# The order of rounding and shifting in the layer norms of a hybrid encoder trunk

## The reference

```python
def layer_norm(x, g, b):
    xf = x.astype(jnp.float32)
    mu = jnp.mean(xf, axis=-1, keepdims=True)
    var = jnp.mean(jnp.square(xf - mu), axis=-1, keepdims=True)
    return ((xf - mu) * lax.rsqrt(var + LN_EPS) * g + b).astype(x.dtype)

for l in range(DEPTH):                                      # DEPTH = 2, D_MODEL = 1024
    x = layer_norm(ALPHA * x + 0.5 * swiglu_ffn(x, ...), ln_g[l, 0], ln_b[l, 0])
    x = layer_norm(ALPHA * x + mix, ln_g[l, 1], ln_b[l, 1])  # mix of even_mixer or odd_mixer
    x = layer_norm(ALPHA * x + 0.5 * swiglu_ffn(x, ...), ln_g[l, 2], ln_b[l, 2])
```

## Time and profile before

| | |
|---|---|
| median of 3 runs | 2367.24 us (2366.89 to 2369.07) |
| the profiled execution | 2367.52 us |
| its span, first to last instruction | 2365.7 us |
| mean granted TensorE clock | 0.998 of full speed |
| TensorE busy | 2340.5 us, 99% |
| VectorE busy | 1701.5 us, 72% |
| ScalarE busy | 1157.2 us, 49% |
| GpSimd busy | 592.3 us, 25% |

### The profile page before, as it was taken

One profiled execution on the slowest core, in us unless ns is written; L12 is line 12 of the kernel. 1 busy time (PEld: TensorE's weight loads), 2 busy tenths in 40 slices (PEclk: granted clock), 3 DMA queues, 4 the chain that ended last, 5 costly groups with the idle time before them and its releaser, 6 DMA issues.

```text
span 2365.7 us, 40265 instructions
## 1 busy us (share of the span) xinstructions
PE 2340.5 (99%) x15948; PEld 2055.4 (87%) x15948; DVE 1701.5 (72%) x2228; ACT 1157.2 (49%) x1664; POOL 592.3 (25%) x310
## 2 busy tenths in 40 slices
PE   9999999999999999999999999999999999999998
PEld 8989987777788989989989988888888888998997
DVE  7818768998779728769728665798987547962857
ACT  5525537985446525536525534455554334552543
POOL 2040044001241030141030144333333334013013
PEclk9999999999999999999999999999999999999999
DMA  5333232232123333223333323222222222333332
GB/s 172 101 108 101 88 114 78 80 87 72 54 88 101 95 109 108 91 88 112 94 99 108 98 98 91 81 72 81 81 81 72 80 77 85 108 94 110 110 98 73
DMA packets 64720, 220.98 MB, mean 93 GB/s; under 512 B 11066, under 2 KB 15674, under 8 KB 64414
## 3 DMA queue, kind: packets, MB, share of 16 engines
q1 hardware_dynamic: 64542, 218.47, 29.8%
HBM read 216.35 MB, written 2.10 MB: 92 GB/s over the span
## 4 chain that ended last, share of the span: by engine, by line
PE 87%; DVE 9%; ACT 1%; issue 1%; POOL 1%; DMA 0%; SPq 0%; ACTq 0%; DVEq 0%
PE ps L735 13%; PE ps L737 13%; PE ps L736 13%; PE ps L920 11%; PE ps L921 11%; PE ps L919 11%; PE ps L717 2%; PE ps L723 2%; PE ps L718 2%; DVE sb_x L2433 1%; PE ps L1374 1%; DVE sb_wl L2567 1%; DVE sb_x L2425 1%; DVE sb_x L2437 1%; PE ps L1433 1%
## 5 line engine op out<-in xcount | busy, mean ns | idle before, releaser
L621 POOL TENSOR_TENSOR sb_low<-sb_src,sb_hi 128x1408 fp32r<-128x1408 f32 x60 | 194.9, 3249 | 1086.3 <-ACT sb_hi L1551 1086.2
L621 POOL TENSOR_TENSOR sb_wl<-sb_raw,sb_wh 128x1024 fp32r<-128x1024 f32 x114 | 284.9, 2499 | 518.6 <-ACT sb_wh L1551 494.8
L2242 DVE TENSOR_TENSOR sb_low<-sb_src,sb_hi 128x1024 fp32r<-128x1024 f32 (+1 forms) x304 | 329.5, 1091 | 71.7 <-ACT sb_hi L1615 60.8
L1615 ACT ACTIVATE sb_hi<-sb_src 128x1024 fp32r<-128x1024 f32 (+1 forms) x304 | 286.1, 947 | 186.0 <-PE ps L921 100.4
L919 PE MATMUL ps<-sb_tt,sb_hi 128*128 128x256 f32 x1216 | 344.1, 283 | 0.0
L920 PE MATMUL ps<-sb_tt,sb_low 128*128 128x256 f32 x1216 | 344.1, 283 | 0.0
L921 PE MATMUL ps<-sb_tt,sb_hi 128*128 128x256 f32 x1216 | 344.1, 283 | 0.0
L1551 ACT ACTIVATE sb_wh<-sb_raw 128x1024 fp32r<-128x1024 f32 x139 | 147.0, 1058 | 253.5 <-PE ps L737 222.2
L920 PE MATMUL ps<-sb_xh,sb_low 128*128 128x256 f32 x912 | 258.1, 283 | 0.0
L921 PE MATMUL ps<-sb_xl,sb_hi 128*128 128x256 f32 x912 | 258.1, 283 | 0.0
L919 PE MATMUL ps<-sb_xh,sb_hi 128*128 128x256 f32 x912 | 258.1, 283 | 0.0
(11 more groups left out here) (419 smaller groups left out, 5116.4 us busy)
## 6 DMA issues: line engine op xcount, KB each, us to landing
sb_src<-w_s SPq DMA_DIRECT2D x76, 768.0 KB, 4.3
sb_src<-w_out SPq DMA_DIRECT2D x64, 704.0 KB, 4.1
sb_raw<-w_od SPq DMA_DIRECT2D x80, 512.0 KB, 3.6
sb_raw<-w_ev SPq DMA_DIRECT2D x40, 512.0 KB, 3.7
sb_src<-w_s SPq DMA_DIRECT2D x76, 256.0 KB, 2.9
sb_src<-w_in SPq DMA_DIRECT2D x16, 512.0 KB, 3.6
sb_raw<-w_evo SPq DMA_DIRECT2D x8, 512.0 KB, 3.6
sb_raw<-w_odo SPq DMA_DIRECT2D x8, 512.0 KB, 3.7
```

The lines of the kernel that those rows point to most:

```text
L621: pool.tensor_tensor(sl.wl[:, 0:n], sl.raw[:, 0:n], sl.wh[:, 0:n].bitcast(F32), ALU.subtract).then_inc(lo_done, 1)
L1615: act.activation(hi[:, lo_:hi_at, :], groups(i)[g], ACT.Copy).then_inc(hi_s[g], 1)
L2242: dve.tensor_tensor(low[:, a_:b_, :], groups(i)[g], hi[:, a_:b_, :].bitcast(F32), ALU.subtract).then_inc(lo_s[g], 1)
```

## The change

Both engines' norms are reordered; the arithmetic of each value stays, except that the rounded part of an odd tile is now made from scaled tile plus bias on ScalarE, as it was for even tiles, and no more copied from the shifted tile. On ScalarE `tile` writes the rounded part of every tile, and a new `shift` adds the bias to `x` for even tiles, three tiles later in the first sequence (`SHIFT_BEHIND`) and one tile later in the second. On VectorE `tile` only scales, and a new `shift` adds the bias for odd tiles, three tiles later in the first sequence (tiles 5 and 7 after tile 7) and one tile later in the second; it waits for the rounded part to be there, since it writes over the tile that ScalarE reads. The low parts of odd tiles now wait for VectorE's shift as well. The last norm keeps its order.

```diff
--- before.py
+++ after.py
@@ -43,6 +43,7 @@
 CW = 32
 BY_ACT = (0, 2, 4, 6)
 BY_DVE = tuple(k for k in range(KD) if k not in BY_ACT)
+SHIFT_BEHIND = 3
 SUB_POOL = (4, 5, 6, 7)
 LOW_DVE = (4, 7)
 LOW_POOL = tuple(k for k in range(KD) if k not in LOW_DVE)
@@ -646,6 +647,8 @@
                     pool.wait_ge(xh_done, KD * g + k + 1)
                     if n and k in BY_ACT:
                         pool.wait_ge(x_act, len(BY_ACT) * (g - SEQS) + upto(BY_ACT, k))
+                    elif n:
+                        pool.wait_ge(x_dve, len(BY_DVE) * (g - SEQS) + upto(BY_DVE, k))
                     pool.tensor_tensor(xl[:, k, part(q)], x[:, k, part(q)], xh[:, k, part(q)].bitcast(F32),
                                        ALU.subtract).then_inc(xl_pool, 1)
 
@@ -1745,15 +1748,16 @@
                 def tile(q, k):
                     m = SEQS * ln + q
                     x_k, h_k, b = x[:, k, part(q)], xh[:, k, part(q)], vc("ln_b", ln * KD + k)
-                    if k in BY_ACT or not more:
-                        act.wait_ge(scaled, KD * m + k + 1)
-                        if more:
-                            act.activation(h_k, x_k, ACT.Identity, bias=b).then_inc(xh_done, 1)
-                            act.wait_ge(xh_done, KD * (m + SEQS) + k + 1)
+                    act.wait_ge(scaled, KD * m + k + 1)
+                    if more:
+                        act.activation(h_k, x_k, ACT.Identity, bias=b).then_inc(xh_done, 1)
+                    else:
                         act.activation(x_k, x_k, ACT.Identity, bias=b).then_inc(x_act, 1)
-                    elif more:
-                        act.wait_ge(x_dve, len(BY_DVE) * m + upto(BY_DVE, k))
-                        act.activation(h_k, x_k, ACT.Copy).then_inc(xh_done, 1)
+
+                def shift(q, k):
+                    m, x_k = SEQS * ln + q, x[:, k, part(q)]
+                    act.wait_ge(xh_done, KD * (m + SEQS) + k + 1)
+                    act.activation(x_k, x_k, ACT.Identity, bias=vc("ln_b", ln * KD + k)).then_inc(x_act, 1)
 
                 def mean(q):
                     act.wait_ge(mean_mm, 3 * ln + 2 + q)
@@ -1770,6 +1774,8 @@
                 rstd(0)
                 for k in range(KD):
                     tile(0, k)
+                    if more and k - SHIFT_BEHIND in BY_ACT:
+                        shift(0, k - SHIFT_BEHIND)
                     if k == 0:
                         last(1)
                     if k == 1:
@@ -1781,9 +1787,12 @@
                     if k == 7:
                         rstd(1)
                 if more:
+                    shift(0, BY_ACT[-1])
                     split(KD, next_slot(ln, 2), stages[ln + 1][1] + 2)
                 for k in range(KD):
                     tile(1, k)
+                    if more and k - 1 in BY_ACT:
+                        shift(1, k - 1)
 
             def head_rstd(c, r, ahead=None):
                 ln_and_exp()
@@ -2432,8 +2441,11 @@
                         dve.wait_ge(sub_done, (own_ + KD) * ln + own_ * q + k + 1)
                     dve.scalar_tensor_tensor(x_k, x_k, vc("ln_g", ln * KD + k), ps[:, VAR_BANK[q], part(q)],
                                              ALU.mult, ALU.mult).then_inc(scaled, 1)
-                    if k in BY_DVE and more:
-                        dve.wait_ge(scaled, KD * m + k + 1)
+
+                def shift(q, k):
+                    if more:
+                        m, x_k = SEQS * ln + q, x[:, k, part(q)]
+                        dve.wait_ge(xh_done, KD * (m + SEQS) + k + 1)
                         dve.scalar_tensor_tensor(x_k, x_k, vc("ln_b", ln * KD + k), zero, ALU.add,
                                                  ALU.add).then_inc(x_dve, 1)
 
@@ -2450,8 +2462,12 @@
                     tile(0, k)
                     if k == 0:
                         last(1)
+                    if k - SHIFT_BEHIND in BY_DVE:
+                        shift(0, k - SHIFT_BEHIND)
                     if k == 5:
                         variance(1)
+                for k in BY_DVE[-2:]:
+                    shift(0, k)
                 for k in range(own_):
                     sub(1, k)
                 if more:
@@ -2462,8 +2478,11 @@
                 dve.wait_ge(rstd_done, 2 * (SEQS * ln + 1) + 2)
                 for k in range(KD):
                     tile(1, k)
+                    if k - 1 in BY_DVE:
+                        shift(1, k - 1)
                     if k == LOW_DVE[0] + 2:
                         low(1, LOW_DVE[0])
+                shift(1, KD - 1)
                 low(1, LOW_DVE[1])
                 dve.wait_ge(scaled, KD * (SEQS * ln + 2))
 
@@ -2472,6 +2491,8 @@
                 dve.wait_ge(xh_done, KD * g + k + 1)
                 if n and k in BY_ACT:
                     dve.wait_ge(x_act, len(BY_ACT) * (g - SEQS) + upto(BY_ACT, k))
+                elif n:
+                    dve.wait_ge(x_dve, len(BY_DVE) * (g - SEQS) + upto(BY_DVE, k))
                 dve.tensor_tensor(xl[:, k, part(q)], x[:, k, part(q)], xh[:, k, part(q)].bitcast(F32),
                                   ALU.subtract).then_inc(xl_dve, 1)
```

## The result

| | before | changed |
|---|---|---|
| median | 2367.24 us | 2377.08 us (2376.89 to 2381.70) |
| ratio to before | | 1.0043, 95% interval 1.0033 to 1.0054 |
| span of the profiled execution | 2365.7 us | 2375.3 us |

The changed kernel is 9.8 us slower. The forecast was 2373.5 with a range to 2376.3: the direction is right, the size is a third too small, and the time lies 0.8 outside the range.

What follows compares the result with a forecast made beforehand. TensorE's queue was taken as the bound, busy 99% of the span. Three feed-forward norms at 3.1 and two mixer norms at 3.2 add 6.3 us to 2367.24: 2373.5, own range 2371.1 to 2375.6, 8-in-10 range 2368.8 to 2376.3.

Steps and rivals of the forecast that it cites:

- walk through the queues: Reordered engine queues followed through a norm: first sequence keeps 0.3, second loses it; 0.98 us lost per feed-forward norm.
- first rival: Identities on ScalarE start 0.31 apart (decides from 0.33 down): loss only 2.6 us, 2369.8, same; chance 0.15.
- VectorE's three waits: Second sequence, before tile 7: VectorE's shift waits for ScalarE's rounded part, 0.25 us three times.
- GpSimd's queue behind the mixers: Low part 0 waits for late shift 0, so the weight's and other low parts come 2 us later; end moves 1.0.
- a weight part off the path: Sign of being wrong: the weight's low part behind the mixers, forecast to make TensorE wait 0.9, is not on the path.
- price of a collision: VectorE's two low parts among GpSimd's behind mixers: 0.1 to half a microsecond each; 1.6 a norm taken, between 1.1 and 2.2.
- 0.54 row: VectorE low part in a GpSimd stream before the change: 0.54 instead of 0.43, held to agree only in part with full exclusion.
- the last low part beside GpSimd's tile 6: Second sequence, feed-forward norms: VectorE's last low part at 77.81 falls beside GpSimd's; next work starts at 80.2 to 80.4.
- the 0.2 for clearing `sb_lum`: Behind stage 0, VectorE's clearing queued behind its last low part adds 0.2 us, making three feed-forward norms 3.1.
- second rival: VectorE and GpSimd exclude each other at full price: 2.3 in two norms, 1.2 to 1.3 in three; 2375.6; chance 0.15.
- 2.63 row: VectorE operation beside a long GpSimd one before the change took 2.63 us, cited in full support of the exclusion.

Runs made afterwards that it cites:

- e3: Changed kernel, but VectorE's low parts of tiles 4 and 7 in the norms subtract zeros in PSUM instead of the rounded part in SBUF: 2373.39 us, 1.0028.
- e10: e5, but VectorE's low parts of tiles 4 and 7 in the norms subtract zeros in PSUM: 2373.53 us, 1.0027.
- e7: Changed kernel, but in the second sequence ScalarE shifts tile 6 before it rounds tile 7: 2380.72 us, 1.0056.
- e9: e6, but in the first mixer's stage GpSimd's next weight operation waits for VectorE's low part of tile 7: 2365.87 us, 0.9993.
- e1: First sequence of every norm as in the changed kernel, second as in the kernel before: 2374.84 us, 1.0031.
- e5: Changed kernel, but behind the two mixers GpSimd makes the second weight tile's low part ahead of low part 0: 2377.33 us, 1.0044.
- e6: e1, but VectorE's shift of tile 7 follows its eight subtractions and GpSimd makes the weight's low part first behind the mixers: 2368.24 us, 1.0005.
- e4: Kernel before, but VectorE's low parts of tiles 4 and 7 subtract zeros in PSUM: 2367.05 us, 1.0000.
- e8: Kernel before, but GpSimd makes the weight's low part ahead of low part 0 behind the two mixers: 2369.74 us, 1.0006.

## Why the prediction was wrong in its size

Point by point, from the lengths. The order alone, counted as the forecast counted it (from the kernel before as measured), is e3 less before, the collisions are the changed kernel less e3:

| us, norm of stage | 0 | 1 | 2 | 3 | 4 | sum |
|---|---|---|---|---|---|---|
| order, forecast | 0.98 | 1.0 | 0.98 | 0.98 | 1.0 | 4.9 |
| order, measured | 0.98 | 1.23 | 1.38 | 1.01 | 1.22 | 5.8 |
| collisions, forecast | 0 | 0.6 | 0 | 0 | 0.6 | 1.2 |
| collisions, measured | 0.38 | 1.16 | 0.64 | 0.16 | 1.16 | 3.5 |

- **Right: the walk through the queues.** In two of three feed-forward norms the order costs 0.98 and 1.01, forecast 0.98. In the norm of stage 2 (4.03 off): the seven first tiles on TensorE end at 67.23 (forecast 67.18, before 67.70), shift 7 at 67.45 (forecast 67.40), the subtractions at 67.85 (67.80), the second sequence on TensorE at 72.60 (72.54); rounded parts in a row start 0.40 apart (two last 0.90, one 0.51), so the first rival's condition is not met. VectorE's three waits are 0.19 each where 0.25 was forecast.
- **Right: GpSimd's queue behind the mixers,** in its times (low part 0 ends at 2013.53, forecast 2006.2 + 7.15 = 2013.35; the weight waits 0.76, forecast 0.9), but it was the wrong reason for a cost: e10 against e3 shows that the late weight is free by itself. The forecast had named a weight part off the path as a sign of being wrong. That its 1.0 came near the 1.23 and 1.22 of order measured there is luck: they stay when the weight is first.
- **Wrong: the price of a collision.** The forecast had 0.1 and half a microsecond for each of the mixers' two low parts, and took 1.6 a norm between 1.1 and 2.2. Measured are 0.5 each and 2.39 and 2.38 a norm: the upper end and a little more. "Between the ends" was the failing choice. The 0.54 row was read as a mild collision; it is in line with the others, a meeting near the end of a GpSimd operation (that one ended at 1075.35, the low part at 1075.63, 0.28 later). The trace of the kernel before had the full price for this very operation, inside GpSimd's ten low parts ahead of the first stage, 0.96 and 0.96:

```profile
12.69 1.84 DVE L2475 TENSOR_TENSOR sb_xl<-sb_x,sb_xh 128x256 fp32r<-128x256 f32 x2
```

This is 1.1 of the miss.
- **Wrong: the collisions left out.** In the second sequences of the feed-forward norms the forecast named the last low part beside GpSimd's tile 6 without a price of its own (its 80.2 to 80.4 leaves it at most 0.2), which is about right (0.16 in stage 3), but it put the low part of tile 4 at nothing, which takes 0.66 in stage 0 and 0.89 in stage 2 and holds up the scaling of tile 7. The three norms make the other 1.2. The meeting in stage 2 follows from the late start in the next point, which the forecast couldn't see.
- **Not foreseen, and in part open:** in the norm of stage 2 VectorE's low part of tile 4 starts 0.34 later than in that of stage 3, without a collision too (e3). The view puts it down to the rounded part of tile 6, for which the code doesn't make it wait. All twelve traces have a gap of 0.40 at one and the same place, between VectorE's 1534th and 1535th instructions (semaphore instructions counted). In the kernel before it lies behind this norm's last low part (1077.08 to 1077.48) and holds up nothing of the norm. The edit puts five more instructions ahead of it, in every kernel here that has the edit or a part of it, and so the 1535th is the low part of tile 4. What the gap is stays open, and no run moved it. With the collision that follows it is why this norm loses 2.02 and that of stage 3, where tile 4's low part takes 0.43, loses 1.17.
- **Wrong, small:** the 0.2 for clearing `sb_lum` behind stage 0 can't be seen: the stretch from that norm to the next is 334.49 before and 334.50 after.

The miss of 3.6 in the time is so 2.3 of collisions and 0.9 of order (0.4 of it the late start, 0.45 the mixers), less the 0.2 for `sb_lum`, and 0.6 that lies outside the five lengths. The second rival was the case: the exclusion at its full price, 2.3 in two norms (measured 2.39 and 2.38) and 1.2 to 1.3 in three (1.36, 2.02 and 1.17). The forecast gave it 0.15. Its 2375.6 is still 1.5 low, by the norm of stage 2 and what lies outside the five lengths. By the Trainium skill (SBUF — State Buffer, section "SBUF: two separate sides") a VectorE operation with two SBUF inputs and a GpSimd operation that reads SBUF exclude each other for the whole instruction. Every collision here agrees, but for some 0.15 us at the end, in which the two overlap (the VectorE row ends 0.28 behind GpSimd's and takes 0.43 alone). The forecast should have taken the rule's end, as the 2.63 row already did.

## What to carry to other kernels

When an edit moves operations of two engines against each other, list every VectorE operation with both inputs in SBUF and every GpSimd operation that can lie beside it, and price the meeting at the rest of the GpSimd operation: a reordering that is right on the path can lose more by a new meeting than it gains (e7), and one wait or one operand in PSUM takes it away (e9, e3). A gain in one sequence must be looked for in each queue that the moved steps share; here 0.5 a norm was real, and a shift placed ahead of eight subtractions gave it back.

## What the runs showed of the hardware

- VectorE's subtraction of 256 columns with both inputs in SBUF takes 0.41 to 0.43 alone. When it met a GpSimd operation that had begun before it and had more than 0.15 to run, it ended 0.28 to 0.29 after that operation's end, whatever its length: 0.89, 0.93, 1.76 for two, 2.33, 2.49 and 2.50 were seen. Where it comes into a gap of GpSimd's it takes 0.43, and GpSimd's row is the longer one (tile 4 in stage 3: five low parts in 3.88, in e3 3.76). With one input in PSUM it takes 0.42 in the same places (mean of 20 in e3: 416 ns).
- The granted clock can fall to the lower level for some 3 us behind TensorE's waits. In a norm it did in e1 (stage 0, after a wait of 1.54), e5 (stage 2, 1.14 and 0.43) and e7 (stage 0, 1.97), and didn't in the changed kernel after waits of 1.14 and 0.41, nor in e6 after 1.56. Ahead of the first norm it did in e4, e8 and e9, after waits of about 2.9. It cost 1.3 in e5. What decides between them stays open.
- VectorE's queue has a gap of 0.40 ahead of its 1535th instruction in all twelve traces, whatever that instruction is; its cause stays open.
